# Modulation vectors from TensorE: fp32 weight tiles fed whole, in four column groups, in a two-block transformer kernel

## The reference

```
c_act = jax.nn.silu(c)                                  # (1, 1024)
for i in range(DEPTH_2):                                # 2 layers
    mod = (c_act @ mod_w[i] + mod_b[i]).reshape(B, 6, D)[:, :, None, :]
    hin = x * (1.0 + mod[:, 1]) + mod[:, 0]             # before the attention
    ...
```

## Time and profile before

| | us |
|---|---|
| median of 3 runs | 1010.79 (1005.18 to 1011.22) |
| the profiled execution, whole | 1007.46 |
| its span, first to last instruction | 1005.7 |
| TensorE busy | 894.0 |
| VectorE busy | 767.2 |
| ScalarE busy | 511.1 |
| GpSimd busy | 369.0 |

### The profile page before, as it was taken

One profiled execution on the slowest core, in us unless ns is written; L12 is line 12 of the kernel. 1 busy time (PEld: TensorE's weight loads), 2 busy tenths in 40 slices (PEclk: granted clock), 3 DMA queues, 4 the chain that ended last, 5 costly groups with the idle time before them and its releaser, 6 DMA issues.

```text
span 1005.7 us, 14200 instructions
## 1 busy us (share of the span) xinstructions
PE 894.0 (89%) x5504; PEld 778.7 (77%) x5504; DVE 767.2 (76%) x1045; ACT 511.1 (51%) x781; POOL 369.0 (37%) x180
## 2 busy tenths in 40 slices
PE   5948998999997898989799999978997889999994
PEld 4946887767675686768699999857996778999993
DVE  4629779788798769678989888889787797555555
ACT  4525455546464654425556556544574465545440
POOL 0414032533114245012615234249242168433425
PEclk9968999999998899898899999979999899999997
DMA  7776654555575475145878777837674287664601
GB/s 291 215 190 223 213 172 149 188 163 178 174 272 177 150 238 210 42 146 181 292 276 278 275 262 264 300 123 265 212 246 148 65 286 267 220 216 165 212 36 42
DMA packets 56715, 201.66 MB, mean 201 GB/s; under 512 B 6732, under 2 KB 7532, under 8 KB 56648
## 3 DMA queue, kind: packets, MB, share of 16 engines
q1 hardware_dynamic: 55672, 198.14, 57.4%
q0 software_dynamic: 976, 2.62, 1.6%
HBM read 198.12 MB, written 2.62 MB: 200 GB/s over the span
## 4 chain that ended last, share of the span: by engine, by line
PE 62%; DVE 23%; issue 5%; ACT 4%; DMA 3%; POOL 3%; POOLq 0%; SPq 0%; DVEq 0%; ACTq 0%
PE ps L990 19%; PE ps L992 18%; PE ps L991 18%; DVE wsp L1194 6%; DVE acc L1253 3%; DMA ring<-in_w_mv 2%; PE ps L1143 2%; PE ps L1164 1%; DVE X L1618 1%; DVE pb L1472 1%; DVE arena L1355 1%; DVE ra L1194 1%; ACT wsp L1726 1%; PE ps L1150 1%; DVE arena L1182 1%
## 5 line engine op out<-in xcount | busy, mean ns | idle before, releaser
L990 PE MATMUL ps<-XT,wsp 128*128 128x256 f32 x768 | 221.5, 288 | 20.9 <-POOL wsp L2026 11.5
L991 PE MATMUL ps<-XT,wsp 128*128 128x256 f32 x768 | 218.0, 284 | 0.0
L992 PE MATMUL ps<-XT,wsp 128*128 128x256 f32 x768 | 217.8, 284 | 0.0
L990 PEld LDWEIGHTS ps<-XT,wsp 128*128 128x128 f32 x768 | 148.7, 194 | 25.2 <-POOL wsp L2026 11.7
L1726 ACT CAST wsp<-ring 128x1024 fp32r<-128x1024 f32 x116 | 121.1, 1047 | 69.9 <-PE ps L992 44.1
L1194 DVE TENSOR_TENSOR wsp<-ring,wsp 128x1024 fp32r<-128x1024 f32 x90 | 144.8, 1615 | 14.1 <-ACT wsp L1726 13.9
L991 PEld LDWEIGHTS ps<-XT,wsp 128*128 128x128 f32 x768 | 148.5, 193 | 1.0
L992 PEld LDWEIGHTS ps<-XT,wsp 128*128 128x128 f32 x768 | 148.5, 193 | 0.0
L1194 DVE TENSOR_TENSOR wsp<-arena,wsp 128x1024 fp32r<-128x1024 f32 (+1 forms) x81 | 128.8, 1593 | 11.2 <-ACT wsp L1726 11.2
L2026 POOL TENSOR_TENSOR wsp<-ring,wsp 128x1024 fp32r<-128x1024 f32 x26 | 69.7, 2681 | 157.6 <-ACT wsp L1726 157.6
L1726 ACT CAST wsp<-arena 128x1024 fp32r<-128x1024 f32 (+1 forms) x92 | 95.7, 1044 | 27.1 <-PE ps L992 26.7
(11 more groups left out here) (264 smaller groups left out, 1941.6 us busy)
## 6 DMA issues: line engine op xcount, KB each, us to landing
ring<-in_mod_w SPq DMA_DIRECT2D x64, 512.0 KB, 4.3
arena<-in_mod_w SPq DMA_DIRECT2D x32, 512.0 KB, 4.5
arena<-in_ffn_o SPq DMA_DIRECT2D x25, 512.0 KB, 4.5
ring<-in_ffn_a SPq DMA_DIRECT2D x23, 512.0 KB, 4.7
arena<-in_ffn_b SPq DMA_DIRECT2D x23, 512.0 KB, 4.5
ring<-in_ffn_b SPq DMA_DIRECT2D x21, 512.0 KB, 4.9
arena<-in_ffn_a SPq DMA_DIRECT2D x21, 512.0 KB, 4.6
ring<-in_ffn_o SPq DMA_DIRECT2D x19, 512.0 KB, 4.4
```

What stands on the lines that cost most here:

```text
L990: pe.matmul(o, l[0], r[0], start=start, stop=False)
L991: pe.matmul(o, l[0], r[1], start=False, stop=False)
L992: return pe.matmul(o, l[1], r[0], start=False, stop=stop)
```

## The change

The sums on VectorE, ScalarE and GpSimd go. For each tile TensorE now issues four plain fp32 matmuls. The stationary operand is `cactr`, in which column k of the activated `c` is repeated 32 times (128 x 32), and the moving operand is a quarter of the raw tile (128 x 256). Quarter j goes to array columns 32j to 32j+31 (`tile_position=(0, 32 * j)`), and so to partitions 32j to 32j+31 of one PSUM bank. The eight tiles of a vector accumulate in that bank, which is held from the first tile to the last. ScalarE copies the bank to `msum` (128 x 256); every partition of a group of 32 holds the same 256 sums. Then a row vector is made by four fp32 matmuls with a column of the identity as broadcast stationary operand, and a column vector by eight fp32 matmuls with a moving operand of one column. The ring has seven slots where it had five, the side task issues the load for the next tile one step ahead, it takes 10 or 11 steps for a vector where it took 16, and the seven rates are about 0.64 of what they were.

```diff
-MOD_PACE = [0.7, 0.9, 0.8, 1.25, 1.0, 0.8, 0.65]
+MOD_PACE = [0.45, 0.58, 0.52, 0.8, 0.65, 0.52, 0.42]
...
-    bank, raw, part, wk = Turn(8), Turn(5), Turn(4), Turn(3)
+    bank, raw, part, wk = Turn(8), Turn(7), Turn(4), Turn(3)
...
+        soon = [load(("mod_w", 0))]
+        for n in range(12):
+            i, m = n // 6, n % 6
+            b = bank.get()
+            for k in range(8):
+                s = soon.pop(0)
+                if n * 8 + k + 1 < 96:
+                    soon.append(load(("mod_w", n * 8 + k + 1)))
+                add("mod_k", i, m, k, s, b, prior("bank", b))
+                free_raw(s)
                 yield
+            add("mod_sum", i, m, b, sums[n % 2])
+            bank.put(b[0])
...
+                elif kind == "mod_k":
+                    i, m, k, s, b, before = a
+                    for e in new("P", ("ld", *s), ("cact", 1), before):
+                        pe.wait_ge(*e)
+                    for j in range(4):
+                        ins = pe.matmul(ps[b[0]][32 * j:32 * j + 32, 0:256], cactr[:, k * 32:(k + 1) * 32],
+                                        raw[s[0]][:, j * 256:(j + 1) * 256], start=k == 0, stop=k == 7,
+                                        tile_position=(0, 32 * j))
+                    ins.then_inc(*done("P", "mod_k", i, m, k, also=[("raw", *s)]))
                 elif kind == "mod_pe":
...
                     if br is not None:
-                        pe.matmul(ps[b[0]], ones_r[:, :], mr[:, 0:512], start=True, stop=False)
-                        ins = pe.matmul(ps[b[0]], ones_r[:, :], mr[:, 512:1024], start=False, stop=True)
+                        for j in (2 * cb, 2 * cb + 1):
+                            ins = pe.matmul(ps[b[0]][:, (j % 2) * 256:(j % 2) * 256 + 256],
+                                            bass.AP(cst, 32 * j, [[NCONST, 128], [0, 128]]), total, start=True, stop=True)
                     else:
...
+                        for k in range(8):
+                            ins = pe.matmul(ps[b[0]][:, k:k + 1], total[:, (k % 2) * 128:(k % 2) * 128 + 128],
+                                            ID[:, 32 * (k // 2):32 * (k // 2) + 1], start=True, stop=True)
...
-                elif kind == "mod_k" and a[2] % 2 == 0:
...
-                        ins = ve.scalar_tensor_tensor(acc[0], raw[s[0]], cact[:, k:k + 1], acc[0], MUL, ADD)
-                    ins.then_inc(*done("V", "mod_a", i, m, k, also=[("raw", *s)]))
...
-                elif kind == "mod_k" and a[2] % 2:
...
-                        ac.activation(raw[s[0]], raw[s[0]], ACT.Copy, scale=cact[:, k:k + 1]).then_inc(
-                            *done("A", "mod_s", i, m, k))
...
+                elif kind == "mod_sum":
+                    i, m, b, before = a
+                    for e in new("A", ("mod_k", i, m, 7), before):
+                        ac.wait_ge(*e)
+                    ac.copy(msum[m % 2], ps[b[0]][:, 0:256]).then_inc(*done("A", "mod_sum", i, m, also=[("bank", *b)]))
...
-                elif kind == "mod_k" and a[2] % 2 and a[2] > 1:
...
-                    po.tensor_tensor(acc[1], acc[1], raw[s[0]], ADD).then_inc(
-                        *done("G", "mod_b", i, m, k, also=[("raw", *s)]))
```

More of the change, by code:

```diff
@@ L306, in modulation @@
     def modulation():
[L307 to L315, removed]
-                yield
[L317 to L336, removed]
-                yield
@@ new lines, in modulation @@
+        sums = [None, None]
+        soon = [load(("mod_w", 0))]
[8 more added lines that the diff above has]
+                free_raw(s)
+                yield
+            add("mod_sum", i, m, b, sums[n % 2])
+            bank.put(b[0])
+            yield
+            is_row, r = m in (2, 5), 0 if m == 2 else 1
+            while i and is_row and ("r2", r) not in have:
+                yield
+            br = load(("row", "mod_b", i * 6144 + m * 1024)) if is_row else None
+            if is_row:
+                yield
+            for cb in range(2 if is_row else 1):
+                b = bank.get()
+                add("mod_pe", i, m, cb, b, prior("bank", b), br)
+                sums[n % 2] = ("mod_pe", i, m, cb)
+                bank.put(b[0])
+            if is_row:
+                free_raw(br)
+            else:
+                add("mod_fin", i, m)
+            have.add(("mod", i, m))
+            yield
@@ L811, in build @@
         R2 = sb("R2", 2048)[:, :].rearrange("p (m n) -> p m n", m=2)
-        acc = [sb(f"acc{i}", 1024)[:, :] for i in range(2)]
+        cactr = sb("cactr", 256)[:, :]
+        msum = [sb(f"msum{i}", 256)[:, :] for i in range(2)]
         small = sb("small", 512)
@@ L867, in build @@
         vv = grid(arena[:, 6400:8448], 2)
-        raw = [ring_t[:, i * 1024:(i + 1) * 1024] for i in range(5)]
+        raw = [ring_t[:, i * 1024:(i + 1) * 1024] for i in range(7)]
         raw += [GTf[:, 0:1024], GTf[:, 1024:2048], mvf[:, 0:1024], mvf[:, 1024:2048], avf, cqf, qrf]
@@ L1244, in vector @@
                         ve.wait_ge(*e)
-                    ve.tensor_scalar(cact, cact, 0.5, None, MUL).then_inc(*done("V", "cact", 1))
-                elif kind == "mod_k" and a[2] % 2 == 0:
[L1247 to L1252, removed]
-                        ins = ve.scalar_tensor_tensor(acc[0], raw[s[0]], cact[:, k:k + 1], acc[0], MUL, ADD)
-                    ins.then_inc(*done("V", "mod_a", i, m, k, also=[("raw", *s)]))
[L1255 to L1260, removed]
+                    ve.tensor_scalar(grid(cactr, 8), bass.AP(small, cact.offset, [[512, 128], [1, 8], [0, 32]]), 0.5, None,
+                                     MUL).then_inc(*done("V", "cact", 1))
                 elif kind == "mod_pe":
@@ L1272, in vector @@
                             ve.wait_ge(*e)
[L1273 to L1276, removed]
+                        y = {0: 0, 1: 8, 3: 16, 4: 24}[m]
+                        ve.tensor_tensor(MC[i][:, y:y + 8], ps[b[0]][:, 0:8], K("mod_b", i * 48 + m * 8, 8), ADD).then_inc(
+                            *done("V", "mod_ev", i, m, 0, also=[("bank", *b)]))
                 elif kind == "mod_fin" and a[1] in (1, 4):
@@ L1280, in vector @@
                     a_, s_ = MC[i][:, x:x + 8], MC[i][:, x - 8:x]
-                    for e in new("V", ("mod_ev", i, m, 1)):
+                    for e in new("V", ("mod_ev", i, m, 0)):
                         ve.wait_ge(*e)
```

36 lines of the change are left out of this document (4 added, 32 removed).

## The result

| | before | changed |
|---|---|---|
| median, 20 runs each | 1006.83 us (1004.46 to 1014.22) | 1010.65 us (1009.65 to 1012.47) |
| profiled execution, whole | 1007.46 us | 1010.07 us |
| its span | 1005.7 us | 1008.3 us |

The ratio is 1.0032, with a 95% interval of 1.0018 to 1.0046. The change costs 4 us by the medians, and 2.6 us between the two profiled spans. The forecast was 1050, off by 40 us; the time lies in the stated range, in its "same" case.

What follows compares the result with a forecast made beforehand. TensorE was taken to bound the kernel, busy 894.0 of 1005.7 us. 1007.46 + 80 (sets) + 3 (end products) - 34 (relief) - 6 (slots) = 1050 us, slower; range 1000 to 1165, to hold 8 in 10.

Steps and rivals of the forecast that it cites:

- "same" case: Whole kernel: time within about 1%, 10 us, of no change; chance 0.08.
- Price of a set: TensorE's four matmuls per tile: groups stream side by side, 0.43 us plus 0.4 for leaving the whole array, 80 us for 96.
- products at the end of a column vector: TensorE's small closing products: 14 us both before and after; with row vectors' products, net +3 us.
- The 80 us lie on the path wherever TensorE is in a full stream: TensorE's 96 tile sets: their 80 us were added in full, as TensorE streams fully for most of the run.
- What they can give back is bounded by the waits of rows 2: Work removed from VectorE, GpSimd and ScalarE: relief limited by TensorE's listed waits, 28 us, plus 6 us of clock, 34 us.
- the upper end named, 60 us: Relief from the other engines: at most about 60 us, all load-dependent TensorE waits and their clock.
- Slots: Two more ring slots and early load: half of an 11.5 us wait in the congested start given back, 6 us.
- Bank, splits, tile waits: Held PSUM bank costs nothing; modulation-sum splits give back 5 us; TensorE's tile waits cost nothing except in the congested start.
- The signs named: Changed profile: TensorE busy near 970 us, VectorE under 675, GpSimd near 237; waits for GpSimd and modulation split gone.
- three signs of being wrong: Set under 0.5 us; TensorE waiting at the new line for tiles or banks; idle time falling much more than 40 us.
- sets fall into idle time: Rival: sets fill TensorE's gaps between weight units and the switch costs half; about 1010 us, chance 0.06.
- relief is larger than TensorE's waits say: Rival: unlisted short waits and layer-norm chains shrink too, about 70 us back, sets only 0.43 us; 982 us, chance 0.08.

Runs made afterwards that it cites:

- a1: Changed kernel with all four matmuls of a tile sent to one column group, number and shape of instructions kept: 1119.58 us, ratio 1.1114.
- e1: Changed kernel with two tile sets at each visit and the side task's rates times 0.6, nothing left out: 1005.15 us, ratio 0.9962.
- c2: Changed kernel without TensorE's sets for tiles 1 to 7; ScalarE touches 8 columns of each instead: 959.24 us, ratio 0.9521.
- b2: Kernel before, modulation work on VectorE, ScalarE and GpSimd cut to 8 columns except each chain's first tile; splits stay: 954.37 us, ratio 0.9468.
- b1: Kernel before with only GpSimd's modulation additions and final sums cut from 1024 columns to 8: 960.82 us, ratio 0.9535.
- e4: Changed kernel with five ring slots and 48 GpSimd additions put back on a tile nobody else uses: 1028.78 us, ratio 1.0192.
- d1: Changed kernel with five own ring slots instead of seven, nothing left out: 1014.65 us, ratio 1.0067.
- b4: Kernel before, modulation work on three engines and the splits of the sums cut to 8 columns, except first ones: 952.97 us, ratio 0.9455.

## Why the prediction was wrong

The forecast was +43 us against the profiled execution, measured are +4. By its own steps:

**Price of a set: right in mechanism, a little high.** Full overlap of the groups was taken, and a1 and the timeline show it. Booked 0.83 us, measured 0.76: 73 us instead of 80 (72 with the four pairs). At the full clock the products at the end of a column vector took 1.62 us before and take 1.70 now, those of a row vector 0.92 and 1.54: for eight and four of them +3 us, as booked. So TensorE got about 76 us, not 83. The switch costs 0.33 us a visit (e1), close to the 0.4 read from the earlier trace rows.

**"The 80 us lie on the path wherever TensorE is in a full stream": this counted the sets in full, and failed.** c2 shows that 80% of the visits' time is time of the kernel. The sets stand at borders between weight units, and a part of them falls where TensorE would have waited for a low part. In the first FFN the sentence is right (21.3 us of sets cost 23.4); it fails before the MLA attention, where 20.5 us of sets cost 9.3. I had this as a rival of 0.06 and as nothing in the sum; it is worth 15 of the 76 us, leaving 61.

**"What they can give back is bounded by the waits of rows 2", sized at 34 us: this is the term that failed most.** b2 gave 53 with the same splits and products. Booked were 28 us of waits, 5 of them for the splits, and 6 for the clock. Measured in b2 are 33.5 us less idle time, where 23 were booked without the splits, and 19 us less busy time, of which the clock is about 15 (32 us less of TensorE's work at the lower level). So the bound itself held: the upper end named, 60 us, covers the 53. What failed is the size of both terms: 33.5 in place of 23 for the waits, and about 15 in place of 6 for the clock. I had looked at one stretch at the lower level and not summed them; the kernel before has 105.6 us of them, with TensorE busy in 71.

What lengthens the waits is named by b1: cutting GpSimd's additions alone gives 47 us. 116 us of GpSimd work cost VectorE 90 us. I had read the slowing in the earlier trace rows and never sized it over the run. It reached the softmax scaling too: booked at 5 of 9.8 us, that wait fell by 8.2 in b1. How much of the 47 is the slowing, how much GpSimd's own late low parts and how much the faster release of slots and sums was not separated in the kernel before; in the changed one the slowing alone is 14 (e4).

**Slots: right.** 6 us booked, 4 measured (d1). **Bank, splits, tile waits:** no wait for a bank shows; the splits are worth 1.4 us at most once the other load is gone (b4), where I booked 5 us, though TensorE's wait for them, 4.6 us before, is 1.9 in b1 already; TensorE does wait for a tile in the congested start, 6.5 us, as feared.

**The signs named.** TensorE's busy time should have been near 970 us and is 943.9: about 20 of the missing 26 us are the clock, the rest the cheaper sets. VectorE's 593.6 and GpSimd's 224.4 are under the 675 and near the 237 named. Two of the three signs of being wrong came: TensorE waits for a tile at the new line, and its idle time fell by 47 us, where much more than 40 was the sign. The third did not, a set costs 0.76 us and not under 0.5.

**The account.** 76 x 0.80 = 61 in, 53 + 4 = 57 out: +4, and the runs say +4. The share of 80% is from c2, where other work than in the whole change was cut; with 71% or 89% the sum would be -3 or +11. So the parts are shown, and that they add so neatly is partly luck. That the sum comes so near to nothing is luck too: two effects of some 60 us each cancel, and nothing ties one to the other.

**The rival that decided.** It is a mixture of "sets fall into idle time" and "relief is larger than TensorE's waits say". Each alone was given under 0.1; nothing in the rows ruled them out together, and the first 450 us show them together, with 14.8 us gained.

## What to carry to other kernels

Before you size a relief, sum two things for the engine that binds: its idle time, and its work in stretches at the lower clock. Closing gaps gave back both here, and the list of waits shows only the first. Work taken from GpSimd can be worth more than the waits for GpSimd when VectorE is nearly full: take one VectorE shape, its mean less its fastest (1.59 and 1.21 us for the low parts here), multiply by its count (214, so 82 us), and treat it as VectorE's load. Work added to the bound engine in small pieces costs less than its length where that engine still waits, and its full length where it doesn't, so count it by stage. If small-tile matmuls are mixed into a full-array stream, put several in one visit, and look whether their loads fall into a stretch in which TensorE then waits for a tile (13.7 us in e1).

## What the runs showed of the hardware

Four fp32 matmuls of 32 stationary and 256 moving columns in four column groups take 0.57 us against 1.84 us in one group, and a second set behind the first adds 0.43 us. Leaving the full array for them costs 0.33 us a visit. Although each fp32 instruction is two records, the four first ones run together and then the four second ones; an instruction's second record doesn't hold up the next group (starts within 0.02 us, then again 0.24 us later). With the same instructions on TensorE and less load on the other three engines, 32 us less of TensorE's work ran at the lower clock (b2: mean granted clock 0.947 to 0.965). 116 us less of GpSimd's fp32 additions took 90 us from VectorE in the kernel before, and 111 us more put 53 us on it in the changed one (e4).
